# Feed-forward up products: three matmuls of 256 columns, or one of 512 and one of 256 with the halves added afterwards

## What is computed

```python
D_MODEL, SEQ, D_FF, CONV_W = 1024, 256, 2816, 3

def swiglu(h, wg, wu, wd):                       # four times, in the first block
    return (jax.nn.silu(h @ wg) * (h @ wu)) @ wd

def conv_ffn(h, w_up, conv_w, conv_b, w_down):   # twice, in the second block
    a, v = jnp.split(h @ w_up, 2, axis=-1)
    a = causal_depthwise_conv(a, conv_w, width=CONV_W) + conv_b
    return (jax.nn.silu(a) * v) @ w_down

x = x + 0.5 * g1 * swiglu(modulate(rms_norm(x, g), sh1, sc1), wg, wu, wd)
```

## Time and profile before

| | us |
|---|---|
| median of three runs | 1808.8 |
| the three runs | 1805.85, 1808.8, 1808.93 |
| span of the profiled execution (first to last instruction) | 1806.0 |
| TensorE busy in it | 1747.5 (97%) |
| VectorE busy | 1382.4 (77%) |
| ScalarE busy | 912.2 (51%) |
| HBM reads | 408.9 MB, 228 GB/s over the span |

### The profile page before, as it was taken

One profiled execution on the slowest core, in us unless ns is written; L12 is line 12 of the kernel. 1 busy time (PEld: TensorE's weight loads), 2 busy tenths in 40 slices (PEclk: granted clock), 3 DMA queues, 4 the chain that ended last, 5 costly groups with the idle time before them and its releaser, 6 DMA issues. The chain is left out here.

```text
span 1806.0 us, 35803 instructions
## 1 busy us (share of the span) xinstructions
PE 1747.5 (97%) x14215; PEld 1709.8 (95%) x14215; DVE 1382.4 (77%) x1621; ACT 912.2 (51%) x1267; POOL 261.5 (14%) x423
## 2 busy tenths in 40 slices
PE   6999999999999999999999999899999998899999
PEld 5999999999999999989999998899999997699999
DVE  6767798687668877767967789769888898778555
ACT  3433377763335433456533366566444556655443
POOL 1411110011002011010110134411110121200000
PEclk9999999999999999999999999999999998999999
DMA  9988857459876888746697847335889492137450
GB/s 347 372 305 277 298 171 256 152 176 327 298 270 233 281 286 289 261 176 221 239 320 258 298 160 252 106 121 198 298 301 286 136 242 98 48 129 256 166 184 24
DMA packets 256071, 411.42 MB, mean 228 GB/s; under 512 B 17975, under 2 KB 200801, under 8 KB 255841
## 3 DMA queue, kind: packets, MB, share of 16 engines
q1 hardware_dynamic: 223032, 290.79, 49.2%
q0 software_dynamic: 32432, 119.04, 17.7%
q10 hardware_dynamic: 504, 0.18, 0.0%
HBM read 408.90 MB, written 2.63 MB: 228 GB/s over the span
## 5 line engine op out<-in xcount | busy, mean ns | idle before, releaser
L2678 DVE TENSOR_TENSOR lo<-raw,hi 128x2048 fp32r<-128x2048 f32 (+1 forms) x257 | 582.0, 2267 | 234.5 <-ACT hi L2512 234.0
L2512 ACT CAST hi<-raw 128x2048 fp32r<-128x2048 f32 (+1 forms) x266 | 498.4, 1876 | 387.2 <-PE dacc L2244 186.1
L2242 PE MATMUL up<-operand_hi,hi 128*128 128x256 f32 x1952 | 554.4, 284 | 3.6 <-DVE lo L2678 3.6
L2243 PE MATMUL up<-operand_lo,hi 128*128 128x256 f32 x1952 | 553.8, 284 | 0.0
L2244 PE MATMUL up<-operand_hi,lo 128*128 128x256 f32 x1952 | 553.6, 284 | 0.0
L2242 PEld LDWEIGHTS up<-operand_hi,hi 128*128 128x128 f32 x1952 | 375.9, 193 | 4.5 <-DVE lo L2678 4.4
L2243 PEld LDWEIGHTS up<-operand_lo,hi 128*128 128x128 f32 x1952 | 376.0, 193 | 0.0
L2244 PEld LDWEIGHTS up<-operand_hi,lo 128*128 128x128 f32 x1952 | 375.9, 193 | 0.0
L2242 PE MATMUL dacc<-act_hi,hi 128*128 128x256 f32 x1056 | 300.6, 285 | 3.4 <-DVE act_lo L2891 3.4
L2244 PE MATMUL dacc<-act_hi,lo 128*128 128x256 f32 x1056 | 299.8, 284 | 0.0
L2243 PE MATMUL dacc<-act_lo,hi 128*128 128x256 f32 x1056 | 299.2, 283 | 0.0
(11 more groups left out here) (432 smaller groups left out, 2784.4 us busy)
## 6 DMA issues: line engine op xcount, KB each, us to landing
ada<-in_ada_w_dram POOLq DMA_DIRECT2D x224, 512.0 KB, 6.0
raw<-in_ffn_wg_dram SPq DMA_DIRECT2D x88, 512.0 KB, 4.9
raw<-in_ffn_wu_dram SPq DMA_DIRECT2D x88, 512.0 KB, 5.3
raw<-in_ffn_wd_dram SPq DMA_DIRECT2D x88, 512.0 KB, 5.1
raw<-in_ffn_w_up_dram SPq DMA_DIRECT2D x88, 512.0 KB, 4.5
raw<-in_ffn_w_down_dram SPq DMA_DIRECT2D x46, 512.0 KB, 4.4
raw<-in_hg_w_in_dram SPq DMA_DIRECT2D x32, 512.0 KB, 6.0
raw<-in_attn_w_qkv_dram SPq DMA_DIRECT2D x24, 512.0 KB, 7.0
```

The source lines that it names most:

```text
L2242: pe.matmul(o, stat[0], mov[0], start=start, stop=False, skip_group_check=True)
L2243: pe.matmul(o, stat[0], mov[1], start=False, stop=False, skip_group_check=True)
L2512: last = act.copy(put(slab(hi, s, SPL)), take(slab(raw, s, RAW)))
L2678: last = dve.tensor_tensor(put(slab(lo, s, SPL)), take(slab(raw, s, RAW)), put(slab(hi, s, SPL)).bitcast(F32), ALU.subtract)
```

## The change

In the feed-forward phases, all gate and up slabs but those of the first block in `raw_first` phases and the first slab behind the normalisation change their form. `operand_hi` and `operand_lo` become the two halves of one tensor. For each 128x128 piece the high weights take both halves as 512 moving columns into a whole PSUM bank (`hi*hi` in columns 0 to 255, `hi*lo` in 256 to 511), and the low weights take `operand_hi` into columns 0 to 255: two matmuls instead of three, 32 a slab instead of 48. `wide_first`, used for the first slab behind the normalisation, keeps 48 matmuls of 256 columns.

The gate now takes both banks of `up`, the up product both banks of `misc`. For each of them ScalarE copies the `hi*lo` halves to SBUF (`gate_tail`, `up_tail`: 128x512) and VectorE adds the other halves from PSUM (`gate_sum`, `up_sum`: 128x512). Silu, taps and product read the sum in SBUF. The new semaphores are `wide_tail` (the copy) and `wide_summed` (the addition). The sums of F2's gain and of the vectors inside the loop move to bank 0 of `up`, with waits of their own; the `ada_sum` after the loop waits for the last `up_sum`. (`x_loaded` is folded into `row_in`, and `weight_ready` goes.)

```diff
+            def wide_product(s, dst):
+
+                sl = (slab(hi, s, SPL), slab(lo, s, SPL))
+                both = operand[:, :].rearrange("p (h k n) -> p h k n", h=2, k=KB)
+                for k in range(KB):
+                    for b in range(2):
+                        w = [t[:, k * SEQ + b * P:k * SEQ + (b + 1) * P] for t in sl]
+                        pe.matmul(bank(dst, b).rearrange("p (h n) -> p h n", h=2), w[0], both[:, :, k, :], start=(k == 0),
+                                  stop=False, skip_group_check=True)
+                        last = pe.matmul(bank(dst, b)[:, 0:SEQ], w[1], op_k(operand_hi, k), start=False, stop=(k == KB - 1),
+                                         skip_group_check=True)
+                last.then_inc(slab_used, 1)
...
             def ffn(p):
                 b = BASE[p]
+                first = 1 if p in raw_first else 0
+
                 def ups(i, it=0):
-                    u = count_up(p, i)
                     for j in range(2):
                         s = b + (3 * i - 1 if i else 0) + j
                         slab_ready(s, it)
-                        if u and not (p in raw_first and isinstance(it, int) and i == 1):
-
-                            pe.wait_ge(S[("silu_done", "prod_done")[j]], u + 2 * it)
-                        col_product(s, bank(up, j), p if (i, j) == (1 if p in raw_first else 0, 0) else None)
+                        if i > first:
+                            pe.wait_ge(S["wide_summed"], 2 * wide_before(p, i) - 1 + j + 4 * it)
+                        if j == 0 and i == 2 and p in gained:
+                            pe.wait_ge(S["row_kept"], gained.index(p) + 1)
+                        if j == 0 and i == 4 and p in five_vectors:
+                            pe.wait_ge(S["mod_done"], FIRST_VEC[p] + 1 + it)
+                        (wide_first if (i, j) == (first, 0) else wide_product)(s, (up, misc)[j], *((p,) if (i, j) == (first, 0) else ()))
...
                 if v is not None:
+                    pe.wait_ge(S["wide_summed"], 2 * wide_before(p, FI))
                     ada_sum(v + 4 if p in five_vectors else v)
                 down(FI - 1, stop=True)
...
+                def gate_tail(s, i, it=0):
+
                     act.wait_ge(slab_used, s + 1 + RAW * it)
-                    if u:
-                        act.wait_ge(S["prod_done"], u + 2 * it)
+                    act.copy(pair_view(gate_first), halves(up)[1]).then_inc(S["wide_tail"], 1)
+
+                def up_tail(s, i, it=0):
+
+                    act.wait_ge(slab_used, s + 2 + RAW * it)
+                    act.copy(pair_view(up_first), halves(misc)[1]).then_inc(S["wide_tail"], 1)
+
+                def silu(i, it=0):
+
+                    act.wait_ge(S["wide_summed"], 2 * wide_before(p, i) + 1 + 4 * it)
+                    if count_up(p, i):
+                        act.wait_ge(S["prod_done"], count_up(p, i) + 2 * it)
...
                     if not ahead:
                         split_hi(a + 2, it)
-                    silu(a, i, it)
+                    gate_tail(a, i, it)
                     split_hi(a + 3, it)
+                    silu(i, it)
                     conv_silu(i, it)
+                    up_tail(a, i, it)
                     split_hi(a + 4, it)
                     hidden_hi(i, it)
...
+                def gate_sum(i, it=0):
+
+                    dve.wait_ge(S["wide_tail"], 2 * wide_before(p, i) + 1 + 4 * it)
+                    dve.tensor_tensor(pair_view(gate_first), halves(up)[0], pair_view(gate_first),
+                                      ALU.add).then_inc(S["wide_summed"], 1)
+
+                def up_sum(i, it=0):
+
+                    dve.wait_ge(S["wide_tail"], 2 * wide_before(p, i) + 2 + 4 * it)
+                    dve.tensor_tensor(pair_view(up_first), halves(misc)[0], pair_view(up_first),
+                                      ALU.add).then_inc(S["wide_summed"], 1)
...
                     if not ahead:
                         split_lo(a + 2, it)
+                    gate_sum(i, it)
                     taps(i, it)
                     k = some(count[0], k)
                     split_lo(a + 3, it)
                     k = some(count[1], k)
-                    product(a + 1, i, it)
+                    up_sum(i, it)
+                    product(i, it)
                     split_lo(a + 4, it)
                     hidden_lo(i, it)
```

More of the change, by code:

```diff
@@ L119, in build @@
         ada_acc = sb("ada_acc", D)
[L120 to L121 removed]
+        operand = sb("operand", 2 * KB * SEQ, F32R)
+        operand_hi, operand_lo = operand[:, 0:KB * SEQ], operand[:, KB * SEQ:2 * KB * SEQ]
         x = sb("x", KB * SEQ)
@@ L273, in build, with gain_place @@
         five_vectors = [p for p in FFNS if p in FIRST_VEC and p != phases[-1]]
+        def gain_place(p):
+            return bank(up, 0)[:, 0:SEQ] if p in FFNS else misc[:, SEQ:2 * SEQ]
         def x_count(p):
@@ L306, in count_up, with wide_before, halves, pair_view @@
             return FFNS.index(p) * FI + i
+        def wide_before(p, i):
+            n = FFNS.index(p)
+            return n * FI - sum(q in raw_first for q in FFNS[:n]) + i - (p in raw_first)
+        def halves(t):
+            v = t[:, :].rearrange("p (b h n) -> p b h n", b=2, h=2)
+            return v[:, :, 0, :], v[:, :, 1, :]
+        def pair_view(t):
+            return t.rearrange("p (b n) -> p b n", b=2)
         def tap(p, w, i, j, it=0):
@@ L2259, in col_product, with wide_first @@
                 last.then_inc(slab_used, 1)
+            def wide_product(s, dst):
[9 more added lines that the diff above has]
+                last.then_inc(slab_used, 1)
+            def wide_first(s, dst, p):
+                sl = (slab(hi, s, SPL), slab(lo, s, SPL))
+                n = normed_count(p) - KB
+                for k in range(KB):
+                    pe.wait_ge(S["norm_hi"], n + k + 1)
+                    for b in range(2):
+                        for q in range(2):
+                            pe.matmul(bank(dst, b)[:, 0:SEQ], sl[q][:, k * SEQ + b * P:k * SEQ + (b + 1) * P],
+                                      op_k(operand_hi, k), start=(k == 0 and q == 0), stop=False, skip_group_check=True)
+                for k in range(KB):
+                    pe.wait_ge(S["norm_lo"], n + k + 1)
+                    for b in range(2):
+                        last = pe.matmul(bank(dst, b)[:, SEQ:2 * SEQ], sl[0][:, k * SEQ + b * P:k * SEQ + (b + 1) * P],
+                                         op_k(operand_lo, k), start=False, stop=(k == KB - 1), skip_group_check=True)
+                last.then_inc(slab_used, 1)
             def first_product(s, dst, p):
@@ L2402, in gain_sum @@
                 pe.wait_ge(S["sqrt_done"], norm_list.index(p) + 1)
-                pe.matmul(misc[:, SEQ:2 * SEQ], ones[:, :], gain_acc, start=True,
+                if p in FFNS:
+                    pe.wait_ge(S["wide_summed"], 2 * wide_before(p, 1) + 1)
+                pe.matmul(gain_place(p), ones[:, :], gain_acc, start=True,
                           stop=True, skip_group_check=True).then_inc(S["sums_g_done"], 1)
@@ L2452, in ffn @@
                         if p in five_vectors and i == 3:
-                            ada_sum(v, it)
+                            pe.wait_ge(S["wide_summed"], 2 * wide_before(p, 3) + 1 + 4 * it)
+                            ada_sum(v, it, bank(up, 0))
                         down(i - 1, it)
                 if v is not None:
+                    pe.wait_ge(S["wide_summed"], 2 * wide_before(p, FI))
                     ada_sum(v + 4 if p in five_vectors else v)
@@ L2635, in ffn @@
                     split_hi(b + 2)
-                    silu(b, 0)
+                    gate_tail(b, 0)
+                    silu(0)
                     split_hi(b + 3)
+                    up_tail(b, 0)
                 conv_silu(0)
@@ L2870, in taps @@
                         dve.wait_ge(S["tap_a"], 2 * c + 2 + 4 * it)
-                        g = (gate_first if isinstance(it, int) and i == 0 else bank(up, 0))[:, j * SEQ:(j + 1) * SEQ]
+                        g = gate_first[:, j * SEQ:(j + 1) * SEQ]
                         o = silu_sb[:, j * SEQ:(j + 1) * SEQ]
@@ L2926, in ffn @@
                     split_lo(b + 2)
+                    gate_sum(0)
                     split_lo(b + 3)
-                    product(b + 1, 0)
+                    up_sum(0)
+                    product(0)
                 hidden_lo(0)
```

32 lines of the change are left out of this document (15 added, 17 removed).

## The result

The changed kernel takes 1817.7 us (median of four runs, 1816.4 to 1818.5); the kernel before, on the same chip, 1808.9. The ratio is 1.0048, 95% interval 1.0034 to 1.0062: slower by 8.9 us, where 4.2 us less were forecast. The profiled execution took 1818.26 us.

The account below looks back on a forecast made before the run. TensorE was taken as the bound, with VectorE near it in C0. Gains of F0 3.0, F1 and F3 2.6 each, F2 0.3, C1 1.45, less C0's 5.75, gave 4.2 us: 1808.8 to 1804.6 us, range 1793 to 1814.

Parts of the forecast that it names:

- The wide matmul, 116 x 0.213 = 24.7 us: TensorE, 116 gate and up slabs: each falls from 5.76 to 5.55 us, 24.7 us saved at most.
- no row shows the two shapes in turns: Wide slabs on TensorE: saving per piece bounded from none to 0.013 us; 0.013 taken from the 512-column rows.
- rival (3): Wide slabs: a wide matmul costs two narrow ones, nothing gained, waits of 15.6 us stay, 1824 us; chance 0.12.
- Nothing lost inside the loops of F0 to F3: Loops of F0 to F3: split a+4 ready at 13.5 us, needed at 16.7, so no wait; 0 us lost.
- 1.45 us before each down(10): Ends of F0 to F3: down(10) waits for `act_lo`, 1.45 us each, 5.8 us in all.
- Rival (2): Longer stops at F2's gate(2), gate(3) and C0's end lower the clock, 2.8 us each; 1810 to 1813; chance 0.20.
- F2, 2.3 us at gate(2): F2's start: gate(2) waits for `row_kept`, behind ScalarE's square root of the gain; 2.3 us lost.
- C0, +5.75 us: C0: late gate(3) leaves 1.4 us, loop rounds add 1.35, the end 3.0; 5.75 us longer, not 4.05 shorter.
- 0.85 gained: Each C0 loop round: 0.85 us gained against 1.3 lost at up(i+1), so +0.45 in three rounds.
- the wait for `mod_done`: gate(4) in the loops of F0 to F3: this new wait is met some 1.7 us early.
- N, 0: Part N, which the change doesn't touch: forecast difference 0 us.
- Rival (1): VectorE and ScalarE do the added work in idle time: all 24.7 us gained, 1784, half the waits 1794; chance 0.12 together.

Follow-up runs that it names:

- e1_narrow: Changed kernel with three matmuls of 256 columns per piece again, copies, sums, waits and order kept; 1833.4 us.
- e6_c1sum: Changed kernel plus a dummy vector sum, result not used, behind up(3) in each round of C1's loop; 1826.0 us.
- e8_mod: Changed kernel with the loop's `mod_vector` moved ahead of split a+4 and `act_lo` on VectorE; 1816.1 us.
- e9_c_old: Changed kernel with C0 and C1 put back to three matmuls, no copies or additions, old order; the change stays in F0 to F3; 1808.5 us.
- e10_best: e9_c_old with, in F0 to F3, VectorE's tiles ahead of `gate_sum` and F2's gain square root ahead of split a+4; 1798.3 us.
- e2_warm: Changed kernel plus six dummy matmuls between the last vector sum and down(10) in F0 to F3; 1819.3 us.

## Why the prediction was wrong, point by point

Two terms failed. The wide matmul was credited with the most that one row allowed, 24.7 us, where it saved about 16. And half clock behind the short stops before down(10) was put at nothing, where it cost 4.4 us in the profiled execution. Together they are 12.8 of the 14.8 us by which the profiled span missed the forecast.

- **The wide matmul, 116 x 0.213 = 24.7 us.** The mechanism was right, the size not: the step "no row shows the two shapes in turns" took the upper bound for all. The traces have 16.3 us, e1_narrow 15.6. This is 8 to 9 us of the miss, and the largest term. The bound was in the text, but the sum used its upper end alone. At 5.65 us a slab the distance of the wide start to the next is 0.236 on the mean, near the 0.235 that rival (3) named as half the gain.
- **Nothing lost inside the loops of F0 to F3.** Right: no stop there. The rounds are 35.5 + 0.2 because of the slabs' length alone.
- **1.45 us before each down(10).** Right in place, releaser and size: 1.4. Left out of the sum was half clock behind it, 1.47 us in F0, F1 and F2, 4.4 us. Rival (2) had the mechanism, but looked for it only at stops of 1.9 us and more. At three of those, F2's gate(2) and gate(3) of C0 and of C1, the changed kernel kept the clock; it fell at the short ones, which the rival left out. In five kernels with these stops (the changed one, e1_narrow, e6_c1sum, e8_mod, e9_c_old), 14 of 20 went with half clock, and its price is about 1.5 us, not 2.8.
- **F2, 2.3 us at gate(2).** The releaser was right, ScalarE's square root; TensorE stood 1.7 us longer than its usual distance, not 2.3, since the root ended 602.51 - 568.4 = 34.1 us after F2's start and not, as forecast, 603.68 + 0.6 - 569.7 = 34.6, and gate(2) itself was reached a little later by the 5.65 us slabs ahead of it. With its two stops, the half clock and eleven slabs of 5.65 us or more F2 is 1.8 us longer, not 0.3 shorter.
- **C0, +5.75 us.** Measured +9.1. The forecast stops are there in place and releaser, the loop's 1.2 to 1.3 a round (1.3) and the end's 3.52 idle (3.7). Too small were three sizes: gate(3) came 3.0 us later in the part than before and not 1.9, the loop's first second block 3.4 us later and not 1.4, and a round took 37.57 us, 1.2 more than before and not 0.45. What failed is "0.85 gained" a round, and the 0.5 gained ahead of the loop: nearly no slab of C0 took 5.55 us, so the 4.05 us that the sum set against the stops were little over 1. And the text looked at the wait for `mod_done` in F0 to F3 only, where it is met early; in C0 it cost 1.5 us. The end is 3.3 us later (3.0 forecast), and 1.3 us came back by luck, since less of down(10) fell into half clock than before (7.24 us and not 8.55). C1, whose loop has the 5.55 us slabs, came within 0.5 us.
- **N, 0.** +3.9 us in the profiled execution, by more half clock inside it. The change doesn't touch N, and none of the ten other runs repeats it. But the medians are 8.9 us apart and the profiled spans 10.6, so the other executions either had most of it too or lost about as much elsewhere; which isn't known.

Terms: 8.4 for the slabs, 4.4 for half clock at the three ends, 3.9 for N and 1.5 for gate(4) of C0, less 1.3 for the clock of C0's down(10), 0.6 and 1.0 in A and G and 0.5 at gate(2), make 14.8; the span is 10.6 us longer where 4.2 less were forecast, 14.8. That they meet so closely is luck, as smaller differences (gate(3) of C0 and C1, H, the last transposes) are not in the list. Rival (1), that the waits are met, is wrong wherever a stop was forecast.

## What to carry to other kernels

A step added to an in-order engine costs what stands behind it in that engine's program, not its own duration: here the same additions in F0 to F3 gave 1808.5 us with the tiles behind them (e9_c_old) and 1798.3 us with the tiles ahead and F2's square root moved forward (e10_best). Where TensorE is the bound, count for every new stop not only its length but also the chance of some 1.5 us of half clock behind it, even at 1.4 us (14 of 20 here, so about 1 us each, an estimate). And where a saving rests on a distance between matmuls that no row shows in that mixture, put the middle of its bounds in the sum, and not the end that a row of one shape alone gives.

## What was not expected of the hardware

- The same 32 matmuls (fp32r, 512 and 256 columns in turns) take 5.55 us or 5.65 us, and the kind holds for a slab or more; one more short matmul ahead moved 28 slabs from the slower kind to the faster. What in TensorE this is stays open. Slabs of 48 matmuls of 256 columns take 5.76 us.
- TensorE fell to 1.2 GHz for 3.4 us at stops of 1.4 us, 14 times of 20, and behind 1.9 to 2.2 us of matmuls of one column without any stop, 16 times of 32; behind 1.7 us of them in the changed kernel's loops never in 16.
- With the stops before down(10) filled (e2_warm) their half clock was gone, but the total was no shorter, and half clock stood at a gate(2) that had none in the other kernels. Whether the filling brought it there isn't shown; a mend like this has to be read over all parts.
